# A two-layer hybrid encoder on eight cores: output segments in four stores, the last norm's square sums on VectorE

## The reference

```python
x = layer_norm(ALPHA * x + gt1 * (merged @ w_o[l]), ln1_g[l], ln1_b[l])
...
f = jax.nn.gelu(causal_dwconv(up_a, conv_ffn[l]) + conv_ffn_b[l]) * up_g
x = layer_norm(ALPHA * x + gt2 * (f @ w_down[l]), ln2_g[l], ln2_b[l])
```

## Time and profile before

| what | value |
|---|---|
| median of the 3 runs shown | 2562.99 us (2558.45 to 2564.17) |
| the profiled execution's own time | 2534.56 us |
| its span on the slowest core (core 0) | 2533.0 us |
| spans of the eight cores | 2526.0 to 2533.0 us |
| TensorE busy | 2406.7 us, 95% of the span |
| VectorE, ScalarE, GpSimd busy | 74%, 52%, 15% |
| granted TensorE clock, mean of core 0 | 0.994 |
| DMA, mean over the span | 102 GB/s |

### The profile page before, as it was taken

How to read it: one execution, slowest core, us unless ns; L and a number is a source line. 1 busy time by engine, 2 the same in 40 slices (tenths; PEclk the granted TensorE clock), 3 DMA queues, 4 the chain that set the end, 5 groups by cost and what they waited for, 6 DMA issues and landing times.

```text
span 2533.0 us, 48900 instructions; the slowest of 8 cores (2526.0 to 2533.0 us)
## 1 busy us (share of the span) xinstructions
PE 2406.7 (95%) x15856; PEld 1536.3 (61%) x15872; DVE 1867.9 (74%) x3716; ACT 1322.4 (52%) x2416; POOL 370.7 (15%) x533
## 2 busy tenths in 40 slices
PE   1999998999999999999999999999999999999996
PEld 0566665666666776777466665566655666556664
DVE  4788768998898668876868557876587865697655
ACT  4544437996743337874533235866353322477633
POOL 0100013002210012003100002100221000120011
PEclk9999999999999999999999999999999999999998
DMA  9685664485685454556854332463046434345302
GB/s 261 116 177 127 141 117 76 120 217 156 142 162 105 87 102 76 102 94 133 155 118 73 68 67 41 68 101 68 9 77 117 82 67 77 58 76 84 67 9 75
DMA packets 78105, 257.80 MB, mean 102 GB/s; under 512 B 7712, under 2 KB 20000, under 8 KB 77856
## 3 DMA queue, kind: packets, MB, share of 16 engines
q0 software_dynamic: 46944, 170.41, 40.9%
q1 hardware_dynamic: 30912, 84.26, 10.5%
HBM read 416.65 MB, written 8.39 MB: 168 GB/s over the span
## 4 chain that ended last, share of the span: by engine, by line
PE 78%; DVE 9%; issue 5%; ACT 4%; DMA 2%; SPq 1%; DVEq 0%; POOL 0%; ACTq 0%; POOLq 0%
PE PS L616 78%; DVE segs L600 2%; ACT segs L573 2%; DVE xT L583 1%; SPq L625 1%; DMA wsl<-wstream 1%; DVE lns L583 1%; DVE rows L583 1%; DMA xT<-xs 1%; DVE xT L600 1%; DVE segs L583 1%; ACT hT L573 1%; DMA rows<-wstream 1%; ACT xT L573 0%; DVE rows L600 0%
## 5 line engine op out<-in xcount | busy, mean ns | idle before, releaser
L616 PE MATMUL PS<-hT,wsl 128*128 128x384 bf16 (+8 forms) x9408 | 1490.2, 313 | 61.6 <-ACT hT L573 53.9
L616 PEld LDWEIGHTS PS<-hT,wsl 128*128 128x128 bf16 x9408 | 913.5, 98 | 550.2 <-issue 73.4
L616 PE MATMUL PS<-big,wsl 128*128 128x384 bf16 (+5 forms) x3744 | 597.3, 313 | 21.5 <-DVE big L583 17.6
L616 PEld LDWEIGHTS PS<-big,wsl 128*128 128x128 bf16 x3744 | 365.9, 98 | 216.6 <-issue 27.6
L625 POOL DMA_DIRECT2D wsl<-wstream x290 | 157.2, 543 | 1449.1 <-PE PS L616 1391.5
L600 DVE SCALAR_TENSOR_TENSOR segs<-segs,vecs_s 128x384 f32<-128x384 f32 (+4 forms) x528 | 304.0, 581 | 81.1 <-ACT segs L573 60.4
L573 ACT ACTIVATE segs<-PS,vecs_s 128x384 f32<-128x384 f32 (+9 forms) x456 | 248.6, 546 | 203.5 <-PE PS L616 192.8
L573 ACT ACTIVATE segs<-PS,hb 128x384 f32<-128x384 f32 (+4 forms) x288 | 156.0, 552 | 363.3 <-PE PS L616 221.4
L573 ACT ACTIVATE segs<-segs,vecs_s 128x384 f32<-128x384 f32 (+4 forms) x528 | 287.3, 582 | 45.7 <-DVE segs L600 20.9
L600 DVE SCALAR_TENSOR_TENSOR segs<-segs,PS 128x384 f32<-128x384 f32 (+4 forms) x288 | 146.1, 520 | 171.9 <-PE PS L616 129.2
L600 DVE SCALAR_TENSOR_TENSOR big<-PS,vecs_s,segs 128x384 bf16<-128x384 f32 (+5 forms) x360 | 208.8, 581 | 50.9 <-PE PS L616 29.4
(11 more groups left out here) (81 smaller groups left out, 1724.8 us busy)
## 6 DMA issues: line engine op xcount, KB each, us to landing
wsl<-wstream POOLq DMA_DIRECT2D x290, 512.0 KB, 6.8
rows<-wada SPq DMA_DIRECT2D x83, 512.0 KB, 5.9
rows<-wstream POOLq DMA_DIRECT2D x34, 512.0 KB, 7.7
big<-wada SPq DMA_DIRECT2D x13, 512.0 KB, 22.4
rows<-xs SPq DMA_DIRECT2D x8, 576.0 KB, 5.6
xT<-xs SPq DMA_DIRECT2D x3, 1536.0 KB, 14.9
y<-xT SPq DMA_DIRECT2D x3, 1536.0 KB, 6.1
rows<-wpool SPq DMA_DIRECT2D x8, 512.0 KB, 4.9
```

What stands on the lines that cost most here:

```text
L616: R.op("pe", lambda e, oa=oa, la=la, ra=ra, st=st, sp_=sp_: e.matmul(oa, la, ra, start=st, stop=sp_), reads=(la, ra), writes=(oa,), signal ...
```

## The change

Three things are changed. In the last ffn each segment's store is made in four DMAs of two channel groups, with a semaphore each, in both runs. In the last segment of the second run (final) the square sums are added on VectorE and not on GpSimd. And in that segment, at step 5, a logarithm of one column of rq is written to a spare tile called warm, which nothing reads.

```diff
@@ Norm
-            def __init__(self, lo, hi, sums):
+            def __init__(self, lo, hi, sums, final=False):
                 self.lo, self.hi = lo, hi
+                self.final = final
...
                 out = self.sq if j == 7 else self.rq[:, 0:n]
-                tt(out, self.rq[:, 0:n], sq[:, 0:n], ALU.add, eng="pool")
+                tt(out, self.rq[:, 0:n], sq[:, 0:n], ALU.add, eng="dve" if self.final else "pool")
+                if self.final and j == 5:
+
+                    act(warm[:, 0:1], self.rq[:, 0:1], AF.Ln)
@@ ffn
-            norms = [Norm(lo, hi, fS) for lo, hi in parts]
+            norms = [Norm(lo, hi, fS, last_out and run == 1 and hi == TT) for lo, hi in parts]
...
-                    src = xT[:, :, lo:hi]
-                    dma("sp", y[:, :, o0:o0 + hi - lo], src, "y%d" % s, 1024 * (hi - lo) * 4, reads=[src])
+                    for q in range(0, 8, 2):
+                        src = xT[:, q:q + 2, lo:hi]
+                        dma("sp", y[:, q:q + 2, o0:o0 + hi - lo], src, "y%d" % (4 * s + q // 2), 256 * (hi - lo) * 4, reads=[src])
@@ build_program
+        warm = sb("warm", [128, 1], F32)
...
-        for n in ["x%d" % i for i in range(6)] + ["y%d" % i for i in range(3)]:
+        for n in ["x%d" % i for i in range(6)] + ["y%d" % i for i in range(12)]:
...
-        R.wait_all("sp", [("y%d" % s, R.val["y%d" % s]) for s in range(3)])
+        R.wait_all("sp", [("y%d" % s, R.val["y%d" % s]) for s in range(12)])
```

## The result

Measured side by side, the changed kernel took 2531.3 us (median of 4 runs, 2530.25 to 2531.78) and the kernel before 2560.72 (4 runs, 2542.44 to 2564.17): a ratio of 0.9899 [0.9851, 0.9947], faster by 1.0%.

The account below looks back on a forecast made before the run. TensorE's matmuls bound the kernel, leaving gains only at the end and the seam. Stores and square sums gave 3.62 us, logarithm and seam 0; taken off the median 2562.99, that is 2559.4, range 2552.5 to 2565.0.

Parts of the forecast that it names:

- What bounds the kernel: Whole kernel: TensorE's matmuls dominate, so gains are possible only at the end and the seam near 1165 to 1230 us.
- The square sums: Last segment: seven adds move from GpSimd to VectorE, only the seventh on the path; 0.43 us gained, bounds 0 to 0.58.
- The logarithm: Last segment, ScalarE: no table load there to move ahead, so worth 0; at worst 1.3 us lost.
- The four stores: End: only the last quarter store stays exposed; 3.62 us less including 0.43 from the square sums, bounds 2.5 to 5.0.
- Rival 3: End: four quarter stores pay their fixed parts in turn, 2.91 us each; 1.5 us slower, 2564.5; chance 0.05.
- The terms taken off the median of the runs shown: Final sum: 3.62 us taken off the median 2562.99, 28 us above the profiled execution, as terms are absolute; 2559.4.
- Off the profiled execution the sum: Whole kernel: 3.62 us taken off the profiled execution's 2534.56, giving 2530.9.
- The seam taken as 0: Between the runs: earlier quarter stores and x load counted as 0; bounds a gain of 2.5 to a loss of 5.2.
- Rival 1: Seam: x load starts 3.6 us sooner, late weight tile gone; another 2.5 us gained, 2556.9; chance 0.27.
- Rival 2: Seam: store 1's quarters slip ahead of the weight loads, 5.2 us lost there; 1.6 us slower overall, 2564.6; chance 0.08.
- Rival 4: Behind the seam: ScalarE's and VectorE's order shifts, TensorE's waits change; 9.1 slower or 16.3 faster; chance 0.10, loss 0.06.
- The fit: Stores: about 2.0 us fixed plus bytes at 436 GB/s; a quarter estimated at 2.9 us, one whole store 5.6.

Follow-up runs that it names:

- first comparison: Four kernels timed beside the kernel before: changed kernel again, kernel before again, stores alone, squares and logarithm alone; the kernel before had median 2541.1 us.
- e18: Changed kernel, but all three stores of the first run in one piece: 2539.0 us, ratio 0.9989 to the kernel before.
- e17: Changed kernel, but first-run stores in four parts of 32 partitions, all leaving after the last ScalarE pass: 2530.9 us, ratio 0.9947.
- e15: Changed kernel, but in the first run segments 2 and 3 are stored in one piece, segment 1 in quarters: 2543.5 us, ratio 0.9995.
- e6: Changed kernel with quarter stores in the second run only, first run in one piece, square sums on GpSimd: 2532.9 us, ratio 0.9967.
- e10: Changed kernel, the second run's first x load held until the next segment's plain sum is done: 2530.8 us, ratio 0.9967.
- e12: Changed kernel, first x load held until GpSimd has added the next segment's last square: 2530.6 us, ratio 0.9956.
- e16: Changed kernel, but in the first run segment 1 is stored in one piece, segments 2 and 3 in quarters: 2531.7 us, ratio 0.9963.
- e1: Changed kernel unaltered, timed again beside the kernel before: 2530.4 us, ratio 0.9962.
- e8: Changed kernel, the second run's first x load held until the next segment's first ScalarE pass, some 15 us later: 2527.79 us, ratio 0.9962.
- e11: e8 with the last two of the last eight ScalarE passes moved to VectorE: 2530.6 us, ratio 0.9969.
- e13: e8's kernel timed once more, beside the unaltered changed kernel on one chip: 2531.4 us, ratio 0.9947.
- e9: Kernel before, one-piece stores, the second run's first x load held until the next segment's first ScalarE pass: 2536.0 us, ratio 0.9991.

## Why the prediction was wrong, point by point

- **What bounds the kernel: half right.** The two places, the end and the seam, are where the gain is. But the seam was read by who waited in one execution. A margin nearly used up without a wait (7.1 us on core 2), and waits for the weight tile on cores 2 and 4 too (1.55 and 2.07 us), were in the same trace and were not looked at.
- **The square sums: right, undersized.** Forecast 0.43, measured 0.89 from the last residual add to the last pass's end (14.60 before, 13.71 after). 0.47 is the add itself; most of the rest is the mean's start behind the second matmul, 0.55 after its end before and 0.18 now, which the sum had not counted.
- **The logarithm: right, 0.** No table load moved.
- **The four stores: right, undersized.** From the last pass's end to the span's end 6.43 became 2.81: a gain of 3.62, where 3.19 was forecast. The issue came 0.08 after the pass (0.07 forecast), but the quarter landed in 2.5 us, not 2.91. Rival 3 (fixed parts in turn) is out: four quarters, and the end 2.81 after the last pass.
- **The terms taken off the median of the runs shown: the step that failed first.** Its reason, that the terms are in engines and a queue that do not depend on the 28 us between that median and the profiled execution, kept all of the 28 us in the forecast, and they were not explained. The changed kernel has none of them: its four runs lie at 2530.25 to 2531.78. In the first comparison the median of the kernel before was 2541.1, so 6.5 us of the 28 belong to its ordinary executions, most of it for the late cores, which the change touches. The other 22 us stay open: the first paragraph tells which later executions took as long, but of the three runs shown neither trace nor clock is on record.
- **Off the profiled execution the sum gave 2530.9**, and the changed kernel took 2531.3. That is partly luck: the end gave 0.9 us more than forecast, and the slowest core came to the end 1.7 us later than in the profile before.
- **The seam taken as 0: the other step that failed.** Its reason, "other cores have no such wait and cap the gain", took one execution's best core for a cap. Which cores are late changes from one execution to the next, and the metric takes the latest. With the seam of the kernel before and the end of the changed one (e18) the kernel takes 2539.0, with segments in parts (e17, same chip, same end) 2530.9: 8.1 us, three times the bound of 2.5 for the gain. In e15 the difference to e17 is 12.6.
- **Rival 1, at the right place, with half of the mechanism.** Its sign (first x load before 1176, late tile gone) came true: the first x load left at 1170.3 to 1176.2, and no tile was late there. The late tile does make a core late where the stores are in one piece (e18's core 4, e6's core 5). But the start of the first x load is not what decides: with quarters it left as late as in before and at most 1.85 us of waiting came of it (e10, e12), or none (e16). And the longest waits were for another transfer, the third x load, 60 us later.
- **Rival 2 (store 1 in the weights' way): out.** No weight tile was late at that place.
- **Rival 4 (the order moves): not seen** as a cost: TensorE's waits for VectorE's last adds are 25.3 us, 17 times, against 25.4 and 16.
- **What the sum leaves open.** In the comparison with e1 the medians differ by 10.7 us (2541.1 and 2530.4): 4.5 at the end, 4.6 of excess (median 7.2 against 2.6), and 1.6 that no run accounts for. The 29 us of the side-by-side run in the first paragraph are more than that; its runs of before at 2558 to 2564 left no trace, and what they lost beyond this is open.

The prediction quoted a rule that speaks against the change: 1 MiB or more in a transfer (the Trainium skill, "DMA: Bandwidth & Descriptors", Rules for kernel authors). The page gives it as the way to the most bandwidth. Here it is the landing that others wait for, and two stores of 1.2 MB in place of eight of 0.3 MB cost 12.6 us on the slowest core (2543.5 in e15, 2530.9 in e17). The fit that the prediction took from the same page is given there for transfers that GpSimd issues; these stores are issued by SP, and the last quarter landed in 2.5 us, not 2.9.

## What to carry to other kernels

Where a profiled execution is much faster than the median, explain the difference before anything else, and do not take it over into a forecast: compare the spans of all cores in every execution, and look, on all cores, for transfers that land shortly before they are wanted, not only for waits. Follow an in-order queue to its end: a store that a load waits for, behind which the next store stands, adds up landing after landing, and the last one pays. A store that someone waits for, at the end of a kernel or ahead of a load into the same place, is worth trying in a few parts; both places gained by it here.

## What the runs showed of the hardware

- The one-piece store of segment 3, 1192 KB, issued beside x and weight loads, landed in anything from 8.7 to 34.6 us. Four parts of 298 KB, from the first issue to the last landing, took 8.1 to 17.1, and 16.6 to 23.2 where the first x load was held (e8, e11, e13). In the two profiled executions of before and after they are alike, 10.6 to 15.0 and 11.2 to 13.8: the difference is in the long cases. The store of segment 2 took 29.6 to 46.4 in one piece and 27.6 to 41.5 in parts.
- Within one execution two neighbouring cores usually fared alike (e15: cores 2 and 3 at 32.6 and 34.6 us, cores 6 and 7 at 13.1 and 12.8). Why neighbours, and why the longest landings came with one piece, was not found; a kernel with the store of segment 3 ahead of the second x load and nothing else changed was not tried.
- ScalarE's wait for the third x load reached TensorE less 6.7 to 7.2 us: 19.52 became 12.37 (e15), 15.16 became 8.42 (e18), 7.40 became 0.67 (e9).
- A quarter of 384 KB with little beside it landed in 2.5 us, where 1536 KB took 6.1.
- An idle 12.37 us of TensorE cost some 2 to 3 us more in the lower clock behind it (granted 0.83 over 40 us on core 3 of e15, 1.00 on core 7). That is an estimate: the 94 matmuls that core 3 lacks, at core 7's 6.2 per us, are 15.2 us.
